# Refilling the first expert-weight slots by halves, using two spare slots twice, and multiplying part of the result before its scale is known

## The reference

```
def run(args):                      # one expert e on its tokens
    hb = hf[tok]
    return (jax.nn.silu(hb @ w1[e]) * (hb @ w3[e])) @ w2[e]
...
x = x + g2 * _hier_moe(h, ...)      # each token goes to 2 of 32 experts
return _rmsnorm(x, final_g)         # x * rsqrt(mean(x*x) + 1e-6) * final_g
```

## Time and profile before

| what | value |
|---|---|
| median of 3 runs (lowest to highest) | 992.87 us (990.92 to 993.38) |
| the profiled execution | 990.85 us |
| its span | 989.0 us |
| PE busy | 806.6 us (82%) |
| DVE, ACT, POOL busy | 331.3, 309.6, 144.2 us |
| the chain that ended last | PE 54%, DMA 32% |
| read from HBM | 296.03 MB |

### The profile page before, as it was taken

One profiled execution on the slowest core, in us unless ns is written; L12 is line 12 of the kernel. 1 busy time (PEld: TensorE's weight loads), 2 busy tenths in 40 slices (PEclk: granted clock), 3 DMA queues, 4 the chain that ended last, 5 costly groups with the idle time before them and its releaser, 6 DMA issues.

```text
span 989.0 us, 12352 instructions
## 1 busy us (share of the span) xinstructions
PE 806.6 (82%) x5144; PEld 525.1 (53%) x5144; DVE 331.3 (33%) x700; ACT 309.6 (31%) x621; POOL 144.2 (15%) x153
## 2 busy tenths in 40 slices
PE   7998788999999999999979998766567665765655
PEld 5856356999997886687857542212112220221213
DVE  3324576567775554459531310001000000100001
ACT  2326365566665556645541300000100000000002
POOL 0011013345443015144400000000000000000000
PEclk9999999999999999999999999888988897789878
DMA  9923964455544565833709699999999999999995
GB/s 356 427 111 105 404 257 171 171 181 192 198 155 149 181 248 208 307 119 133 285 23 405 252 403 397 427 429 427 427 427 427 431 426 429 425 428 427 430 427 223
DMA packets 23678, 297.94 MB, mean 301 GB/s; under 512 B 2752, under 2 KB 3008, under 8 KB 5440
## 3 DMA queue, kind: packets, MB, share of 16 engines
q1 hardware_dynamic: 23616, 297.09, 74.4%
HBM read 296.03 MB, written 1.05 MB: 300 GB/s over the span
## 4 chain that ended last, share of the span: by engine, by line
PE 54%; DMA 32%; DVE 6%; ACT 5%; POOL 1%; issue 1%; SPq 0%; DVEq 0%; POOLq 0%
PE ps L186 54%; DMA ring<-in_exps 32%; ACT ar L200 1%; POOL ar L217 1%; DVE ar L206 1%; ACT yT L200 1%; ACT ar L197 1%; DVE fr L206 1%; DMA ring<-in_win 0%; DVE yT L214 0%; DVE misc L600 0%; DVE yT L206 0%; DVE rb L266 0%; DVE hT L214 0%; ACT fr L197 0%
## 5 line engine op out<-in xcount | busy, mean ns | idle before, releaser
L186 PE MATMUL ps<-ring,sq 128*32 128x512 f32 x976 | 138.6, 706 | 79.6 <-DMA ring<-in_exps 79.3
L186 PE MATMUL ps<-fr 128*128 128x256 f32 (+1 forms) x852 | 146.1, 327 | 5.9 <-DVE fr L206 4.1
L186 PE MATMUL ps<-ring,ar 128*32 128x512 f32 (+3 forms) x792 | 105.4, 621 | 47.4 <-DMA ring<-in_exps 38.7
L186 PEld LDWEIGHTS ps<-fr 128*128 128x128 f32 x852 | 126.4, 193 | 21.1 <-DVE fr L206 3.5
L186 PEld LDWEIGHTS ps<-ring,sq 128*32 128x32 f32 x976 | 29.9, 120 | 177.0 <-DMA ring<-in_exps 121.7
L186 PE MATMUL ps<-hT,ring 128*128 128x256 f32 (+2 forms) x416 | 93.3, 385 | 6.7 <-DMA ring<-in_win 6.7
L206 DVE TENSOR_TENSOR ar<-ar,ps 128x512 f32<-128x512 f32 x9 | 6.2, 688 | 257.4 <-PE ps L186 257.4
L186 PEld LDWEIGHTS ps<-hT,ring 128*128 128x128 f32 (+2 forms) x416 | 78.1, 189 | 20.7 <-DMA ring<-in_win 6.7
L186 PEld LDWEIGHTS ps<-ring,ar 128*32 128x32 f32 (+1 forms) x792 | 27.5, 120 | 108.8 <-DMA ring<-in_exps 63.4
L186 PE MATMUL ps<-ar 128*128 128x512 f32 (+9 forms) x320 | 67.2, 442 | 18.1 <-DVE ar L206 8.9
L206 DVE TENSOR_TENSOR fr<-ring,fr 128x512 fp32r<-128x512 f32 x79 | 66.2, 855 | 44.2 <-ACT fr L197 44.0
(11 more groups left out here) (194 smaller groups left out, 927.8 us busy)
## 6 DMA issues: line engine op xcount, KB each, us to landing
ring<-in_exps SPq DMA_DIRECT2D x90, 2048.0 KB, 31.0
ring<-in_modw SPq DMA_DIRECT2D x12, 2048.0 KB, 9.0
ring<-in_wup SPq DMA_DIRECT2D x11, 2048.0 KB, 10.1
ring<-in_win SPq DMA_DIRECT2D x5, 2048.0 KB, 8.8
ring<-in_wdown SPq DMA_DIRECT2D x5, 2048.0 KB, 8.2
ar<-in_exps SPq DMA_DIRECT2D x3, 2048.0 KB, 12.7
ring<-in_wo SPq DMA_DIRECT2D x2, 2048.0 KB, 9.8
ring<-in_wgate SPq DMA_DIRECT2D x2, 2048.0 KB, 8.5
```

The costliest lines, as they stand in the source:

```text
L186: return pe(lambda e: e.matmul(o, l, r, start=start, stop=stop, skip_group_check=True), *waits, inc=inc)
```

## The change

Four things are changed.

1. **Halves.** A W1 or W3 piece is now laid out block by block (`w.ap(2048 * kk_ + 512 * q, 512)`), so the first four matmuls read its first half and the last four its second. Pieces 12 and 13 are loaded as two DMAs of 1 MB each: the first waits for the first four matmuls of the piece that was in the slot (`free_half`), the second for all eight.
2. **Gathers.** `first_gather(1)` now stands between the two halves of piece 0, and 2 alone between pieces 0 and 1.
3. **Two places used twice.** Pieces 17 and 18 go to the memory of pieces 8 and 9, once these are used up. The ring slots that they took before go to 19 and 20, and so on: 19 waits for 10, 20 for 11, 21 for 12, 22 for 13.
4. **End.** After c = 1 of the last group the first 512 columns are finished, and DVE multiplies both of their banks by `final_g` there (`t_gain`). At the end ACT multiplies these two by the reciprocal, DVE does the other two banks as before, and two DMAs of 512 KB go out instead of four of 256 KB.

```
+                dst = self.mem = ring[:, i * SLOT:i * SLOT + n]
+                if halves:
+                    uses[i] += 2
+                    h = n // 2
+                    sp.dma(lambda e: e.dma_start(dst[:, 0:h], src[:, 0:h]), s_ring[i], 16 * uses[i], half_freed[i])
+                    self.ready = sp.dma(lambda e: e.dma_start(dst[:, h:n], src[:, h:n]), s_ring[i], 16 * uses[i], freed[i])
+                    return
...
         def expert_slot(j):
-            return placed[j] if j in placed else stream("exps", j)
+            if j in placed:
+                return placed[j]
+            if j in (17, 18):
+                return stream("exps", j, extra=(f"again{j}", placed[j - 9].parts[0][2:], placed[j - 9].done))
+            return stream("exps", j, halves=j in (12, 13))
...
-                    for p in {1: (1, 2), 2: (3,)}.get(j, ()):
+                    for p in {1: (2,), 2: (3,)}.get(j, ()):
                         t_first[p] = first_gather(p)
...
-                                   w.ap(1024 * q + 512 * kk_, 512), k == 0, k == 7, w.ready,
+                                   w.ap(2048 * kk_ + 512 * q, 512), k == 0, k == 7, w.ready,
                                    t_xg[g, k // 4] if g else t_first[k // 2], read[hbk],
-                                   inc=int(kk_ == 1 and q == 3))
+                                   inc=int(q == 3))
+                        if kk_ == 0:
+                            w.free_half(t)
+                        if j == 0 and kk_ == 0:
+                            t_first[1] = first_gather(1)
                     w.free(t)
...
             w.free(last_columns(c, 256 * c, 256, w.i * SLOT, w.ready))
+            if c == 1:
+                t_gain = [v_tt(sq[:, 1024 * j:1024 * j + 512], bank(YB[2 * j]), ar[:, FROW:FROW + 512], ALU.mult,
+                               t_sq[j][-1], t_rows, t_used[last]) for j in range(2)]
...
+        def write_rows(sp, done, j, *waits):
+            o = 1024 * j
+            sp.dma(lambda e: e.dma_start(out[:, o:o + 1024], sq[:, o:o + 1024]), done, 16, *waits)
+
+        t_r = row_roots(act, dve, t_sq)
+        for j in range(2):
+            o = sq[:, 1024 * j:1024 * j + 512]
+            write_rows(sp, s_out, j, a_copy(o, o, t_r, t_gain[j], scale=whole[:, 4 + j:5 + j]), scaled(dve, j, 1, t_r, t_used[last]))
```

More of the change, by code:

```diff
@@ L140, in build, with __init__ @@
         freed = [None] * RING
+        half_freed = [None] * RING
         turn = [0]
         class Slot:
-            def __init__(self, src, n, extra=None):
+            def __init__(self, src, n, extra=None, halves=False):
                 if extra is not None:
@@ L157, in __init__ @@
                 self.i = i
+                dst = self.mem = ring[:, i * SLOT:i * SLOT + n]
[5 more added lines that the diff above has]
+                    return
                 uses[i] += 1
-                dst = self.mem = ring[:, i * SLOT:i * SLOT + n]
                 self.ready = sp.dma(lambda e: e.dma_start(dst, src), s_ring[i], 16 * uses[i], freed[i])
@@ L169, in free, with free_half, stream @@
             def free(self, token):
+                self.done = token
                 if self.i is not None:
                     freed[self.i] = token
-        def stream(name, j, n=SLOT, extra=None):
-            return Slot(A[name][j][:, 0:n], n, extra)
+            def free_half(self, token):
+                if self.i is not None:
+                    half_freed[self.i] = token
+        def stream(name, j, n=SLOT, extra=None, halves=False):
+            return Slot(A[name][j][:, 0:n], n, extra, halves)
         read = [None] * 8
@@ L1709, in build, with row_roots @@
             last_columns(3 + n, 768 + 128 * n, 128, lo, t)
-        def write_rows(act, dve, sp, done, t_sq, *waits):
+        def row_roots(act, dve, t_sq):
             parts = part.rearrange("p (j i) -> p j i", i=8)[:, :, 0:5]
@@ L1714, in write_rows, with scaled @@
             t = act(lambda e: e.activation(whole[:, 2:4], whole[:, 0:2], ACT.Sqrt, bias=eps, scale=1.0 / 1024), t, t_eps)
[L1715 to L1724, removed]
+            return dve(lambda e: e.reciprocal(whole[:, 4:6], whole[:, 2:4]), t)
+        def scaled(dve, j, n, *waits):
+            o = 1024 * j + 512 * n
+            return dve(lambda e: e.scalar_tensor_tensor(
+                out=sq[:, o:o + 512], in0=bank(YB[2 * j + n]), scalar=whole[:, 4 + j:5 + j],
+                in1=ar[:, FROW + 512 * n:FROW + 512 * n + 512], op0=ALU.mult, op1=ALU.mult), t_rows, *waits)
+        def write_rows(sp, done, j, *waits):
[5 more added lines that the diff above has]
+            write_rows(sp, s_out, j, a_copy(o, o, t_r, t_gain[j], scale=whole[:, 4 + j:5 + j]), scaled(dve, j, 1, t_r, t_used[last]))
         o_out = sem("o_out")
@@ L1782, in overflow @@
                                 k = 2 * s_ + kk_
-                                o = i * SLOT + 1024 * q + 512 * kk_ + 128 * m
+                                o = i * SLOT + 2048 * kk_ + 512 * q + 128 * m
                                 t = omm(ps[:, m // 2, (m % 2) * S:(m % 2) * S + S] if hbk == 0 else
@@ L1830, in overflow @@
                                                                         accum_out=part[:, 8 * j + n:8 * j + n + 1]), t2, t_sq[j][0]))
-            write_rows(act, dve, sp, o_out, t_sq, (s_out, 64))
-            return (o_out, 64)
+            t_r = row_roots(act, dve, t_sq)
+            for j in range(2):
+                write_rows(sp, o_out, j, [scaled(dve, j, n, t_r, (s_out, 32)) for n in range(2)])
+            return (o_out, 32)
         ends = [(q.sem, q.count) for q in (pe, act, dve, pool)]
@@ L1860, in _ @@
             sp.emit(e)
-            e.wait_ge(s_out, 64)
+            e.wait_ge(s_out, 32)
         @block.tensor
@@ L1986, in lay_out @@
         w = L[nm].reshape(NE // 4, 4, 4, 2, 128, 512)
-        ex[:, 4 * i:4 * i + 4] = w.transpose(0, 2, 4, 1, 3, 5).reshape(NE // 4, 4, 128, 4, 1024)
+        ex[:, 4 * i:4 * i + 4] = w.transpose(0, 2, 4, 3, 1, 5).reshape(NE // 4, 4, 128, 4, 1024)
     ex[:, 8:12] = L["exp_w2_2"].reshape(NE // 4, 4, 4, 128, 1024).transpose(0, 2, 3, 1, 4)
```

## The result

| | before | after |
|---|---|---|
| median | 992.55 us (12 runs, 990.92 to 995.14) | 988.25 us (12 runs, 985.66 to 990.31) |
| ratio | | 0.9957, 95% interval 0.9947 to 0.9966 |
| the profiled execution, its span | 990.85, 989.0 us | 990.28, 988.6 us |

What follows compares the result with a forecast made beforehand. Bytes were taken to bound the stream from about 620 us; 4.3 us from halves and places plus 1.0 at the end made 5.3, from 990.85 to 985.55 profiled, 987.6 median. Likely band 986.0 to 989.5, range 984.3 to 991.0.

Steps and rivals of the forecast that it cites:

- What binds: Stream from about 620 us: bytes at 428 GB/s set the end, so a queue further ahead there moves the end equally.
- A DMA's fixed part: A DMA finding the queue empty takes 3.4 to 3.7 us more than its data; each later term turns on it.
- that rival: Pieces 12 and 13: halves run one by one, 5.9 us each, 22 is 5.5 late, 997.4 us; chance 4%.
- The 2.0 us and 78%: Skill page's objection to halves: about 2.0 us fixed per DMA, 1 MB at 78% of the rate; sum no change.
- Halves and gathers: Pieces 12 and 13: earlier half loads land piece 16 1.4 to 3.3 us sooner, 2.3 taken; the gather move counts nothing.
- Two places: Pieces 17 and 18 issued earlier, so nothing starves after 16; brings 2.0 us of the 4.3 at piece 22.
- End: Last output: shared final multiplications and two larger DMAs gain 0 to 1.9 us; 1.0 taken.
- unexplained delay: Last output DMA before the change: landed 3.8 us after 984.8 while the others took 2.6, so 1.2 extra.
- 988.6 if the end of the writing binds anyway: Last output landing: stays at its old time of 988.6, so the new end gains 0.
- The sign that I had named: Output end: the prediction is wrong if the output lands more than 5 us after the first is issued.
- The clock at the end: Rival: PE meets the end of the stream at a lower clock, costing 1.9 us in all: 989.5; chance 15%.
- The 2.0 between profile and median: Whole time: the median stands 2.0 us above the profiled execution, unplaced and kept, so 985.55 becomes 987.6.

Runs made afterwards that it cites:

- halves_only: The kernel before with pieces 12 and 13 by halves and gather 1 moved, without reused places, old end: 992.79 us against 992.34, ratio 1.0003.
- no_branch: The changed kernel without the branch to the overflow code on PE, ACT, DVE and SP: 988.16 us from 6 runs, ratio 0.9957.
- end_only: The kernel before with the new end alone: 992.57 us, ratio 1.0002; last output 15.95 us after c = 2.

## Why the prediction was right, and where not

- **What binds** (right). The stream is bound by bytes from piece 20 on, and a shift of the queue at 22 reaches the end: 3.2 us less at 22, 3.6 less at c = 2 and at the end of the span.
- **A DMA's fixed part** (too large for halves). I used 3.4 to 3.7, and the halves of 12 took 5.3 and 5.2, so 2.8 above their 2.45 of data. That made 12 land 0.6 earlier than predicted. The second half of 13 landed 2.45 behind the first, so the halves did not run one by one; that rival is out. The 2.0 us and 78% that the prediction takes from the Trainium skill (DMA: Bandwidth & Descriptors, Anatomy of one DMA and Bandwidth) stand there for DMAs issued by GpSimd, which the prediction does not say. These are issued by SP, and the 2.8 is measured.
- **Halves and gathers** (mechanism right, size off). 2.3 were predicted at piece 16, 1.5 measured: 13 landed within 0.2 of the forecast, but the three pieces behind it took 16.3, not 15.7, with the gap of 6.2 before 15 among them. The sign "no gap over 5.3 us between landings up to 22" was missed: 13, 15 and 19 have 5.8, 6.2 and 5.33. The sentence that the halves' gain would be lost without the places was right to the letter (`halves_only`, ratio 1.0003). The gathers' move is worth nothing, as said.
- **Two places** (right; it is nearly all of the gain). 2.0 predicted; from 16 to 22 there are 1.65 in after, and the places alone bring 1.8 at 22, 2.9 at c = 2, and ratios of 0.996 and 0.997. I credited 2.3 to the halves and 2.0 to the places, as if they added. They do not: the halves alone bring 0, and the places alone most of it (2.9 of 3.6 us in the trace). And one place does what two do, which the same reckoning (20 could land at 50.7, and its turn was later) would have told beforehand.
- **End** (wrong). "I take 1.0, between": it is 0.0. The step that failed is the 1.2 us of "unexplained delay", which I split in half. It is the delay that sets the end. The last output lands 15.8 after c = 2 whether it is issued at 12.0 (before) or at 10.7 (after), and 1.8 us goes with the branch in `no_branch`. The last fetches ahead of that landing begin 14.1 to 14.7 after c = 2 in all thirteen profiles with the branch, with either end; that they are what holds it is not shown. My other end, "988.6 if the end of the writing binds anyway", was the case. The sign that I had named came too: the output lands 5.8 us after the first is issued, not under 5.
- **The clock at the end** (not met). From the landing of c = 2 to the first output's issue all fourteen profiles have 10.0 to 10.3 us. The clock that did vary was piece 0's, which the sum took for granted.
- **The 2.0 between profile and median** (kept, and it served, but without a reason). The profile of before was one of the three with an early piece 0, so it lay 1.7 below its median. After's profile, with 990.28, lies 2.0 above its own.

Sum: 4.3 of stream and 1.0 of end predicted, 3.6 and 0 in the trace, 4.3 (3.4 to 5.3) in the time. The 0.7 between trace and time is open. That the measured 4.3 is the very number of the stream's term is chance, since its two parts came out otherwise.

## What to carry to other kernels

When a transfer queue runs dry in several places in a row, the gains of mending them do not add: mend the last one first, since time won ahead of it is given back there; count for each piece when it could land by its issue and when by its turn. A buffer used once more was worth the wait for issue that it removed, and the first removed all of it. And before shortening the work ahead of the last DMA, look at what else stands in the DMA record behind it.

## What the runs showed of the hardware

- With a branch at the end of the program the last output lands 1.8 us later (5.1 against 3.3 from issue, two DMAs of 512 KB), and six instruction fetches stand beside it. The Trainium skill (Runtime: NRT & Kernel Launch, Instruction fetch mechanics) names the fetch that a taken branch can force as a stall of the engine that branches; here it is the landing of a data DMA that is late. No run shows a stall of the engine.
- Every gap over 5.2 us between landings of the full queue (31 in 14 profiles, 4.9 is usual) has an instruction fetch in it or in the 1 us ahead; no gap without one is over 4.92.
- A DMA of 1 MB that finds nothing queued (the first half of 12) lands 5.0 to 5.4 us after its issue, and one of 2 MB (12) 8.5 to 8.6. With one piece still ahead, 17 and 19 took 8.1 to 8.5, and once 9.8 (17 in `end_only`).
- The same code reaches piece 0 at 552.7 or 554.5 to 556.4 us, and then runs it in 3.6 or 1.9 us. The two could account for most of the 2 to 4 us by which runs of one kernel differ; that was not tried.
